# Paged cache of a latent-attention decoder step: cached pages loaded in two layouts instead of transposed on chip

## The chip, the cores and the metric

One core of a Trainium2 chip runs the whole step as one program. The metric is device time of the program in microseconds (us), the median of several executions.

## The reference

One layer of a hybrid decoder, in fp32, for a prompt of 512 tokens and, with the same weights, 8 sample sequences of 8 new tokens each, which have 2048 cached tokens behind them. The layer is: half an FFN, a combined input projection, a convolution branch (A) and a latent attention branch (B), a gated merge, half an FFN. The change touches only the attention of the sample sequences over the cache:

```
ckv = concat(cache_ckv[pages].reshape(2048, 256), ckv_new)   # 16 pages of 128 tokens, by page_table
kpe = concat(cache_kpe[pages].reshape(2048, 32),  kpe_new)
k   = rmsnorm(concat(ckv @ w_uk per head, kpe for all heads))  # per head, 64 + 32 channels
s   = (q . k) * SCALE, causal;  p = softmax(s)
o   = (p @ ckv) @ w_uv per head                                # the latent rows are also the values
```

## The kernel before

**Stages.** FFN 1 (0 to about 400 us), input projections and convolution (to about 640), prompt attention (to about 708), the sample sequences over the cache (708 to 1015), merge, output projection, FFN 2. Matrix products run as three fp32r products of a rounded copy ("hi") and what is left of it ("lo"): hi*hi, hi*lo, lo*hi.

**The cache stage** goes over 8 sequences (`sequences`, L506: sequence 0, a loop for 1 to 4, then 5, 6, 7), each 16 pages in 8 pairs (`pp`). Cached rows `c_nat` come token by channel, one DMA a page, and rope keys `kpe_nat` token by rope channel, another. The pages' numbers are loaded by SyncE from a table (`page_of`, L722). Two halves of `c_nat` (b = 0, 1) alternate between sequences.

For a pair of pages:
- TensorE transposes four 128x128 blocks of `c_nat` into a PSUM bank (`transpose_pair`, L1750), one pair ahead of use;
- ScalarE copies the bank rounded to `cT_hi` (`pages_hi`, L1272), VectorE subtracts, PSUM minus `cT_hi`, to `cT_lo` (`pages_lo`, L2473);
- TensorE multiplies page by page with `kq`, in which the expanded key weights (512 columns) and the absorbed queries (64 columns) stand side by side: 12 matmuls of 288 columns a page (L1868). PSUM banks for pages alternate in two pairs, so page t waits until ScalarE has read page t-2;
- ScalarE copies the scores to `s_buf` (L1327) and squares the keys to `sq` (L1333); VectorE sums the squares per head (L2655).

For a group of four pages the rope keys are transposed by TensorE in one block (`kpe_transpose`, L1815), copied by ScalarE (`kpe_copy`, L1309), and multiplied with the rope queries (`kpe_scores`, L1825); VectorE adds that to the scores (L2663).

**Softmax and values of the sequence before** (r = s - 1) are interleaved as steps of generators (`soft_pe`, `soft_act`, `soft_dve`; each `next(soft)` runs one step at a set page). VectorE: inverse key norms (L2514 to L2519), scaling of the scores (L2524), maxima (L2529, L2532), shift (L2537, L2538). ScalarE: square root (L1286) and exponentials (L1294 to L1299), each with its table load. For sequences 0 to 5 (r) the values are made in hi and lo parts: ScalarE rounds a pair of pages to `c_hi` (`pair_high`, L1303) and GpSimd subtracts, SBUF minus SBUF, to `c_lo` (`split_pair`, L908) in place of `c_nat` (the first four pages go to `c_lo_first`); GpSimd also makes the low parts of the probabilities (L920, L922). The value matmuls (L1778, L1779) stand in two clusters of 16, ahead of pages 12 and 15. The values of the last two sequences are plain fp32 (L1799).

**Other work in the stage**: convolution steps on VectorE (`late_tap`, L2225, both tensors in SBUF) in sequences 1 to 4, layer norm of branch A in 5 to 7.

**Order.** Every engine runs its own instruction list in the order written; waits are on semaphore counts. SyncE alone issues the page DMAs, in order: for sequence 0 eleven pages of `c_nat` early, the rest when `w_uk` is split; for sequence s from 2 on, a group when the splits or the value matmuls of sequence s-2 have used the slot (`load_pages`, L728). Behind them SyncE issues `w_uv` and the merge weights (L758 to L765). `w_uk` and `w_uv` share their place (S3) with `kpe_nat` and `c_lo_first`; `w_uv` is loaded a second time for the end.

Of the kernel before, what the change touches and what calls it, by code (L numbers as in the profile page):

```python
# [22 lines left out]
P = 128  # L23
# [70 lines left out]
def layer(nc, x_t, cols_in, cache_ckv, cache_kpe, state_conv, page_table, w, const, out):  # L94

    ctx = ExitStack()
    with ctx:
# [25 lines left out]
        ones = keep("ones", [P, P], F32)  # L123
        causal = keep("causal", [P, P], F32)
# [110 lines left out]
        c_lo_first = place("c_lo_first", [P, NP // 4, KL], F32R, S3 + 4096)  # L235
        c_lo = place("c_lo", [P, 2, NP, KL], F32R, A0)
# [87 lines left out]
        first_ckv_in, first_kpe_in = [sem(f"first_ckv_in{b}") for b in range(2)], [sem(f"first_kpe_in{b}") for b in range(2)]  # L324
        both_in = [[sem(f"both_in{b}{g}") for g in range(1, NP // 4)] for b in range(2)]
        ckv_in, kpe_in = ([[first[b], *both_in[b]] for b in range(2)] for first in (first_ckv_in, first_kpe_in))

        def landed_pages(g, uses):

            return uses * (128 if g else 64)  # L330

        ct_tr, ct_hi, ct_lo = sem("ct_tr"), sem("ct_hi"), sem("ct_lo")
        page_mm, page_sq, page_red = (sem(n) for n in ("page_mm", "page_sq", "page_red"))

        pe_tr, pe_copied, pe_scored, scores_copied, scores_read = (sem(n) for n in ("pe_tr", "pe_copied", "pe_scored", "scores_copied", "scores_read"))
# [191 lines left out]
        def page_lo(b, t):  # L527

            return c_lo_first[:, t, :] if t < NP // 4 else c_lo[:, b, t, :]
# [63 lines left out]
        def _(sp):  # L593
# [128 lines left out]
            def page_of(s, t):  # L722
                return sp.value_load(pages[0:1, ds(s * NP + t, 1)], min_val=0, max_val=cache_ckv.shape[1] - 1)

            def load_page(src, dst, landed, page, b, t):
                sp.dma_start(dst[:, b, t, :], src[0, ds(page, 1), :, :].rearrange("a p c -> (a p) c")).then_inc(landed[b][t // 4], 16)

            def load_pages(s, b, used=None, split=None):  # L728
                for g in range(NP // 4):
                    if used is not None and g == 0:  # L730
                        sp.wait_ge(split_made, split)
                    elif used is not None:
                        sp.wait_ge(pages_used, used + 2 * (g + 1))
                    for t in range(4 * g, 4 * g + 4):
                        page = page_of(s, t)
                        load_page(cache_ckv, c_nat, ckv_in, page, b, t)
                        load_page(cache_kpe, kpe_nat, kpe_in, page, b, t)

            AHEAD = 11
            sp.wait_ge(prep_q, 1)  # L740
            for t in range(AHEAD):
                load_page(cache_ckv, c_nat, ckv_in, page_of(0, t), 0, t)
            sp.wait_ge(prep_tr, 2)
            sp.wait_ge(uk_split, 1)
            for t in (4, 5, 6, 7, 0, 1, 2, 3):
                load_page(cache_kpe, kpe_nat, kpe_in, page_of(0, t), 0, t)
            for t in range(8, NP):
                page = page_of(0, t)
                if t >= AHEAD:
                    load_page(cache_ckv, c_nat, ckv_in, page, 0, t)  # L750
                load_page(cache_kpe, kpe_nat, kpe_in, page, 0, t)
            sp.wait_ge(prep_mm, 2)
            load_pages(1, 1)
            with sp.Fori(1, NS // 2) as i:
                for b in range(2):
                    load_pages(i * 2 + b, b, i * (2 * PAIRS) + (EARLY_PAIRS + PAIRS * (b - 2)), i * (2 * SPLITS) + (SPLITS * (b - 2) + 2))

            sp.wait_ge(lat_mm, STACKED)  # L758
            sp.dma_start(w_uv[:, :, :], w["w_uv"][0].rearrange("(k p) h d -> p k (h d)", p=P)).then_inc(late_in, 16)
            for t in range(2):  # L760
                load_merge(t)
            sp.wait_ge(page_mm, NS * NP)
# [28 lines left out]
        def _(pool):  # L791
# [116 lines left out]
            def split_pair(r, b, j):  # L908

                two = slice(2 * j, 2 * j + 2)  # L910
                pool.wait_ge(p_done, high_made(r, j))
                pool.tensor_tensor(c_lo_first[:, two, :] if j < 2 else c_lo[:, b, two, :], c_nat[:, b, two, :],
                                   c_hi[j % EARLY_PAIRS][:, :, 0:KL].bitcast(F32), ALU.subtract)\
                    .then_inc(split_made, 1)
# [10 lines left out]
            def squares(s, b, uses, prev, nxt):  # L925
# [10 lines left out]
                for g in range(NP // 4):  # L936
                    pool.wait_ge(kpe_in[b][g], landed_pages(g, uses))
                if prev:
                    pool.wait_ge(kpe_red, s)
                k = kpe_nat[:, b].rearrange("p t d -> p (t d)")  # L940
                pool.tensor_tensor(ta[:, 0:NP * DR], k, k, ALU.mult).then_inc(kpe_sq, 1)
# [13 lines left out]
        def _(act):  # L955
# [347 lines left out]
            def pair_high(r, b, j):  # L1303

                act.wait_ge(ct_tr, r * PAIRS + (j + 1))
                act.wait_ge(pages_used, r * PAIRS + (j + 1))
                act.activation(c_hi[j % EARLY_PAIRS][:, :, 0:KL], c_nat[:, b, 2 * j:2 * j + 2, :], ACT.Copy).then_inc(p_done, 1)

            def kpe_copy(s, g):  # L1309

                act.wait_ge(pe_tr, s * 4 + (g + 1))
                if not (isinstance(s, int) and s == 0 and g < 2):
                    act.wait_ge(pe_scored, s * 4 + (g - 1))
                act.activation(kpeT[:, g % 2, :], ps[:, PEB, 4 * HQ:4 * HQ + P], ACT.Copy).then_inc(pe_copied, 1)

            def act_seq(s, b, uses, prev, nxt):
                soft = soft_act(s - 1, 1 - b) if prev else None
                for pp in range(NP // 2):
                    if pp + 1 < NP // 2 or nxt:
                        pages_hi(s * (NP // 2) + (pp + 1), (pp + 1) % 2)  # L1320
                    if pp == 4 and nxt:
                        queries_hi(s + 1, 1 - b)
                    for u in range(2):
# [10 lines left out]
                        if t == kpe_page(s, t // 4):  # L1334
                            kpe_copy(s, t // 4)
                        if prev and t in (1, 8, 9):
                            next(soft)
                        if prev and stacked(s):
                            if 2 <= t < 2 + EARLY_PAIRS:
                                pair_high(s - 1, 1 - b, t - 2)  # L1340
                            if t - LATE_AT in (0, 1):
                                for j in range(2):
                                    pair_high(s - 1, 1 - b, EARLY_PAIRS + 2 * (t - LATE_AT) + j)
# [72 lines left out]
        def _(pe):  # L1416
# [333 lines left out]
            def transpose_pair(s, b, uses, pp):  # L1750

                n = s * (NP // 2) + pp
                if pp % 2 == 0:
                    pe.wait_ge(ckv_in[b][pp // 2], landed_pages(pp // 2, uses))
                if not (isinstance(s, int) and s == 0 and pp < 2):
# [1027 lines left out]
```

## Time and profile before

| | us |
|---|---|
| median of 3 runs (1528.05 to 1530.12) | 1528.22 |
| the profiled execution | 1529.87 |
| its span, first to last instruction | 1528.0 |
| TensorE busy (99% of the span) | 1513.9 |
| VectorE busy (69%) | 1055.5 |
| ScalarE busy (43%) | 659.7 |
| GpSimd busy (29%) | 448.2 |

How to read it: PE is TensorE's matmuls, PEld its weight loads, DVE VectorE, ACT ScalarE, POOL GpSimd, SP SyncE; an SPq row is an issue by SyncE's queue. A row `out<-in xN` is a group of N instructions; "idle before" is the time the engine waited, with what ended the wait. Matmuls are pipelined and their ends are modelled, so their times overlap and a busy TensorE is not one at its peak. The chain of waits goes back from the last instruction to what released each step. The granted clock is 0.997 over the span, 1.0 being 2.4 GHz.

### The profile page before, as it was taken

The numbers are of one execution on the slowest core, as the hardware profiler recorded it, in microseconds if no ns is written. First come the engines' busy times: TensorE is split into PE (matmuls) and PEld (weight loads), VectorE is DVE, ScalarE is ACT, GpSimd is POOL, SyncE is SP. The second block draws the span as 40 slices with busy tenths as digits, with TensorE's granted clock in tenths as the row PEclk, the third lists the DMA queues.
The fourth block names the chain that finished last, engine by engine and source line by source line (L and its number), as shares of the span: only waits on it lengthen the run. The fifth ranks groups of instructions, "written<-read, shape, count | busy, mean of one in ns | idle before, by whom it ended". The sixth has DMA issues, their size and how long they took to land.

```text
span 1528.0 us, 31401 instructions
## 1 busy us (share of the span) xinstructions
PE 1513.9 (99%) x11059; PEld 1463.9 (96%) x11059; DVE 1055.5 (69%) x1738; ACT 659.7 (43%) x1247; POOL 448.2 (29%) x463
## 2 busy tenths in 40 slices
PE   8999999999999999999999999999999999999999
PEld 8999999999999999588999999988999999999999
DVE  6999898422269975865877787864659998985000
ACT  6444445322221241364666666662434544444111
POOL 4000002454455743320233333223551000005432
PEclk9999999999999999999999999999999999999999
DMA  6233334232323571002322222312222333332322
GB/s 176 70 97 98 94 90 123 66 95 76 82 75 96 94 119 48 1 1 61 76 67 60 66 63 63 89 56 71 83 82 67 99 96 89 103 95 80 90 76 82
DMA packets 239316, 122.82 MB, mean 80 GB/s; under 512 B 37041, under 2 KB 236146, under 8 KB 239218
## 3 DMA queue, kind: packets, MB, share of 16 engines
q1 hardware_dynamic: 238354, 121.09, 29.6%
q8 instruction: 55, 0.90, 0.2%
q10 hardware_dynamic: 864, 0.48, 0.1%
q14 instruction: 43, 0.35, 0.1%
HBM read 117.95 MB, written 3.58 MB: 80 GB/s over the span
## 4 chain that ended last, share of the span: by engine, by line
PE 67%; issue 21%; POOL 7%; DVE 2%; ACT 2%; DMA 1%; SPq 0%; POOLq 0%; ACTq 0%; DVEq 0%
PE ps L490 29%; PE ps L1506 14%; PE ps L1868 11%; POOL w_lobuf L465 7%; PE ps L1760 1%; PE ps L1631 1%; PE ps L1685 1%; PE ps L1660 1%; PE ps L1799 1%; PE ps L1778 1%; PE ps L1828 1%; PE ps L1779 1%; DMA w_rawbuf<-in_ffn_w_gu 1%; PE ps L476 1%; PE ps L1675 1%
## 5 line engine op out<-in xcount | busy, mean ns | idle before, releaser
L465 POOL TENSOR_TENSOR w_lobuf<-w_rawbuf,w_hibuf 128x256 fp32r<-128x256 f32 (+1 forms) x328 | 316.9, 997 | 798.7 <-ACT w_hibuf L458 798.5
L1506 PE MATMUL ps<-xs,w 128*128 128x288 f32 x3192 | 427.4, 296 | 0.8 <-DVE w L1994 0.8
L1506 PEld LDWEIGHTS ps<-xs,w 128*128 128x128 f32 x3192 | 426.8, 188 | 1.3 <-issue 1.3
L458 ACT ACTIVATE w_hibuf<-w_rawbuf 128x1024 fp32r<-128x1024 f32 (+1 forms) x89 | 104.4, 1172 | 348.1 <-PE ps L490 332.9
L2202 DVE SCALAR_TENSOR_TENSOR xT<-ps,xT 128x576 f32<-128x576 f32 x23 | 17.4, 757 | 202.4 <-PE ps L490 202.4
L1994 DVE TENSOR_TENSOR w<-w_raw,w 128x512 fp32r<-128x512 f32 x228 | 153.5, 688 | 1.0 <-ACT w L1006 0.8
L490 PE MATMUL ps<-a_hi,w_lobuf 128*128 128x288 f32 x682 | 147.5, 297 | 0.0
L490 PE MATMUL ps<-x_hi,w_hibuf 128*128 128x288 f32 x656 | 142.6, 299 | 4.6 <-POOL w_lobuf L465 2.7
L490 PE MATMUL ps<-a_hi,w_hibuf 128*128 128x288 f32 x682 | 147.2, 296 | 0.0
L490 PE MATMUL ps<-a_lo,w_hibuf 128*128 128x288 f32 x682 | 145.4, 294 | 0.0
L490 PE MATMUL ps<-x_lo,w_hibuf 128*128 128x288 f32 x656 | 141.3, 297 | 0.0
L490 PE MATMUL ps<-x_hi,w_lobuf 128*128 128x288 f32 x656 | 141.3, 297 | 0.0
L1006 ACT ACTIVATE w<-w_raw 128x512 fp32r<-128x512 f32 x228 | 131.9, 624 | 6.0 <-DVE w_raw L1988 2.4
L1868 PE MATMUL ps<-kq_hi,cT_hi 128*128 128x288 f32 x512 | 117.6, 311 | 1.3 <-ACT sq L1333 0.8
L490 PEld LDWEIGHTS ps<-x_hi,w_hibuf 128*128 128x128 f32 x656 | 105.8, 189 | 6.4 <-POOL w_lobuf L465 4.0
L2225 DVE SCALAR_TENSOR_TENSOR y<-ext,cols,y 128x512 f32<-128x512 f32 x120 | 108.8, 906 | 4.1 <-DVE y L2225 1.4
L490 PEld LDWEIGHTS ps<-a_hi,w_hibuf 128*128 128x128 f32 x682 | 110.2, 189 | 0.0
L1868 PE MATMUL ps<-kq_lo,cT_hi 128*128 128x288 f32 x512 | 109.4, 295 | 0.0
L1868 PE MATMUL ps<-kq_hi,cT_lo 128*128 128x288 f32 x512 | 109.3, 295 | 0.0
L490 PEld LDWEIGHTS ps<-a_lo,w_hibuf 128*128 128x128 f32 x682 | 109.3, 188 | 0.0
L490 PEld LDWEIGHTS ps<-a_hi,w_lobuf 128*128 128x128 f32 x682 | 109.0, 188 | 0.0
L1018 ACT ACTIVATE ta<-ta 128x576 f32<-128x576 f32 x38 | 26.1, 687 | 189.3 <-DVE ta L2093 189.3
(343 smaller groups left out, 2729.6 us busy)
## 6 DMA issues: line engine op xcount, KB each, us to landing
w_raw<-in_ffn_w_gu SPq DMA_DIRECT2D x76, 256.0 KB, 2.9
up_rows<-in_ffn_w_gu SPq DMA_DIRECT2D x72, 256.0 KB, 3.1
c_nat<-in_cache_ckv SPq DMA_DIRECT2D x128, 128.0 KB, 2.0
w_rawbuf<-in_w_in SPq DMA_DIRECT2D x58, 256.0 KB, 3.2
w_rawbuf<-in_ffn_w_down SPq DMA_DIRECT2D x32, 384.0 KB, 4.1
w_rawbuf<-in_ffn_w_down SPq DMA_DIRECT2D x32, 320.0 KB, 3.4
w_rawbuf<-in_ffn_w_gu SPq DMA_DIRECT2D x24, 256.0 KB, 3.4
w_rawbuf<-in_w_out SPq DMA_DIRECT2D x16, 256.0 KB, 3.2
```

Of the source, the lines that this page charges most:

```text
L458: act.activation(w_hibuf[:, r % HIS, 0:size], w_rawbuf[:, r, 0:size], ACT.Copy).then_inc(w_hi_done, 1)
L465: ins = pool.tensor_tensor(w_lobuf[:, r, part], w_rawbuf[:, r, part], w_hibuf[:, r % HIS, part].bitcast(F32), ALU.subtract)
L476: mm = pe.matmul(ps[:, 2 * s + h, 0:HALF], a, b[:, k, h * HALF:(h + 1) * HALF], start=False, stop=i == len(kts) - 1 and j == 2)
L490: mm = pe.matmul(ps[0:width, 2 * s + h, 0:HALF], a, b[:, k, h * HALF:(h + 1) * HALF], start=first and i == 0 and j == 0, stop=last and i = ...
L1006: act.activation(w7[b][:, slot, 0, :], src, ACT.Copy).then_inc(w7_hi, 1)
L1018: act.activation(ta[:, :], ta[:, :], ACT.Silu).then_inc(gate_act, 1)
L1506: mm = pe.matmul(ps[:, seven_bank(f, slot), 0:HALF], m, xs[:, slot, n, k, :], start=k == 0 and j == 0, stop=k == KH - 1 and j == 2)
L1631: mm = pe.matmul(ps[0:n, 2 * s + b, 0:QL], qaT[k][:, i * P:i * P + n], w_uq[:, k, b * QL:(b + 1) * QL], start=k == 0, stop=k == QL // P - 1)
L1868: mm = pe.matmul(ps[:, page_banks(t) + half, 0:KQ], a, m[:, half, cols], start=k == 0 and j == 0, stop=k == 1 and j == 2)
L1994: dve.tensor_tensor(w7[b][:, slot, 1, :], w7_raw[b][:, slot, 1, :], w7[b][:, slot, 0, :].bitcast(F32), ALU.subtract).then_inc(w7_lo, 1)
L2202: dve.scalar_tensor_tensor(x2, unit(s), scale, x2, op0=ALU.mult, op1=ALU.add).then_inc(x_done, 1)
L2225: dve.scalar_tensor_tensor(dst, src, cw, dst, op0=ALU.mult, op1=ALU.add).then_inc(conv_p_step, 1)
```

## The change

The host hands over the cached pages in three arrays: `pages_t` (page, 128 channels, 2 x 128 tokens), `pages_in` (page, token, 256 latent and 32 rope channels) and `pages_k` (page, 32 rope channels, 128 tokens). The kernel no longer gets `cache_ckv` and `cache_kpe`.

- `c_ring`, 8 slots of a page in the place of `w_uk` and `w_uv`, receives `pages_t`. `pages_hi` and `pages_lo` read it instead of PSUM. A group of four pages takes half the ring; it is loaded when `ct_lo` shows the half's pairs split.
- `kpeT` receives `pages_k` directly, four DMAs of 32 partitions a group; `kpe_transpose` and `kpe_copy` go, `kpe_scores` waits for the DMA.
- `c_nat` has rows of 288 and receives `pages_in`, for values and for the squares of the rope keys, which GpSimd now makes in place. `c_lo_first` goes; all of `c_lo` is made in place.
- `transpose_pair` goes with all its calls. ScalarE's `pages_hi` waits for the ring's DMA and for the matmuls of the pair before the last.
- SyncE issues three DMAs a page and loads four page numbers ahead of each group's waits. Its order within a group: ring, rope keys, rows. `w_uv`'s second load moves behind the last `cT_lo`.
- Small tiles are moved to other places (`diag`, `top`, `mx`, `o_lat`, `den_sum`, `o_all[0]`, ...).

```diff
+        c_nat = place("c_nat", [P, 2, NP, KL + DR], F32, A0)
+        RING = 8
+        c_ring = place("c_ring", [P, RING, KL], F32, S3)
+        c_lo = place("c_lo", [P, 2, NP, KL + DR], F32R, A0)
...
+            def load_ring(g, found):
+                for u, page in enumerate(found):
+                    sp.dma_start(c_ring[:, (4 * g + u + RING // 2) % RING, :], pages_t[ds(page, 1), :, :].rearrange("a p c -> (a p) c"))\
+                        .then_inc(ring_in[g % 2], 16)
+            def load_rows(b, g, found):
+                for u, page in enumerate(found):
+                    sp.dma_start(c_nat[:, b, 4 * g + u, :], pages_in[ds(page, 1), :, :].rearrange("a p c -> (a p) c")).then_inc(nat_in[b][g], 16)
+            def load_kpe(g, found):
+                for u, page in enumerate(found):
+                    sp.dma_start(kpeT[u * DR:(u + 1) * DR, g % 2, :], pages_k[ds(page, 1), :, :].rearrange("a d t -> (a d) t")).then_inc(kpe_in[g % 2], 16)
+            def load_pages(s, b, used=None):
                 for g in range(NP // 4):
+                    found = [page_of(s, 4 * g + u) for u in range(4)]
+                    sp.wait_ge(ct_lo, s * PAIRS + (2 * g - 2))
+                    load_ring(g, found)
+                    sp.wait_ge(pe_scored, s * (NP // 4) + (g - 1))
+                    load_kpe(g, found)
+                    if used is not None:
                         sp.wait_ge(pages_used, used + 2 * (g + 1))
+                    load_rows(b, g, found)
...
+            sp.wait_ge(rows_done, 2 * NT + PT_TILES)
+            found = [page_of(0, u) for u in range(4)]
+            load_ring(0, found)
+            load_kpe(0, found)
             sp.wait_ge(prep_q, 1)
+            load_rows(0, 0, found)
+            for g in (1, 2):
+                load_rows(0, g, [page_of(0, 4 * g + u) for u in range(4)])
             sp.wait_ge(prep_tr, 2)
             sp.wait_ge(uk_split, 1)
+            found = [page_of(0, 4 + u) for u in range(4)]
+            load_ring(1, found)
+            load_kpe(1, found)
+            load_rows(0, 3, [page_of(0, 12 + u) for u in range(4)])
...
             sp.wait_ge(lat_mm, STACKED)
-            sp.dma_start(w_uv[:, :, :], ...).then_inc(late_in, 16)
             for t in range(2):
                 load_merge(t)
+            sp.wait_ge(ct_lo, NS * PAIRS)
+            sp.dma_start(w_uv[:, :, :], ...).then_inc(late_in, 16)
...
-                pool.tensor_tensor(ta[:, 0:NP * DR], k, k, ALU.mult).then_inc(kpe_sq, 1)
+                k = c_nat[:, b, :, KL:KL + DR]
+                pool.tensor_tensor(k, k, k, ALU.mult).then_inc(kpe_sq, 1)
...
-            def pages_hi(n, b):
-                act.wait_ge(ct_tr, n + 1)
-                act.activation(cT_hi[:, b, :], ps[:, b, :], ACT.Copy).then_inc(ct_hi, 1)
+            def pages_hi(s, pp):
+                act.wait_ge(ring_in[pp // 2 % 2], (s * 2 + (pp // 4 + 1)) * 64)
+                if not (isinstance(s, int) and s == 0 and pp < 2):
+                    act.wait_ge(page_mm, s * NP + (2 * pp - 2))
+                act.activation(cT_hi[:, pp % 2, :], ring_pair(pp), ACT.Copy).then_inc(ct_hi, 1)
...
-                tr.then_inc(ct_tr, 1)          # transpose_pair, all of it
-                    .then_inc(pe_tr, 1)        # kpe_transpose, all of it
+                pe.wait_ge(kpe_in[g % 2], (s * 2 + (g // 2 + 1)) * 64)     # kpe_scores
...
-                dve.tensor_tensor(cT_lo[:, b, :], ps[:, b, :], cT_hi[:, b, :].bitcast(F32), ALU.subtract).then_inc(ct_lo, 1)
+                dve.tensor_tensor(cT_lo[:, pp % 2, :], ring_pair(pp), cT_hi[:, pp % 2, :].bitcast(F32), ALU.subtract).then_inc(ct_lo, 1)
```

## Rows read from the trace of the kernel before

**Rows 1.** Busy times by stretch: sequence 1, 5, 6.
```profile
core 0: us, PE busy (x) PEld busy (x) DVE busy (x) ACT busy (x) POOL busy (x), PEclk, DMA share, GB/s
745.40:782.70 37.30, 37.03 (x281) 35.90 (x279) 29.08 (x50) 25.43 (x63) 14.36 (x12) 1.00 0.22 57
...
894.70:935.40 40.70, 38.94 (x287) 37.19 (x286) 31.25 (x54) 27.12 (x68) 14.81 (x12) 1.00 0.23 59
935.40:972.80 37.40, 36.60 (x279) 35.60 (x277) 29.99 (x50) 26.23 (x66) 14.32 (x12) 1.00 0.25 64
```

**Rows 2.** Chain of waits in sequence 0: start, us, engine, line.
```profile
725.34 0.11 PE ps L1822
725.45 0.44 PE ps L1760 x4
725.88 3.17 PE ps L1868 x24
```

**Rows 3.** Chain of waits in sequence 2, pages 8 and 11.
```profile
801.43 0.34 ACT L1294
...
804.53 1.59 PE ps L1868 x10
```

**Rows 4.** Chain of waits in sequences 5 and 7.
```profile
906.77 2.08 DVE mx L2529
...
999.11 7.05 PE ps L1799 x32
```

**Rows 5.** Chain of waits at the start of sequence 0.
```profile
708.35 1.04 PE ps L1760 x4
```

**Rows 6.** Busy times by stretch: just before sequence 0.
```profile
704.40:707.80 3.40, 3.40 (x19) 3.40 (x17) 2.45 (x5) 0.00 (x0) 0.00 (x0) 0.50 0.08 12
```

**Rows 7.** Timeline of VectorE, sequence 2: start, us, instruction, idle before.
```profile
789.28 0.69 DVE L2475 TENSOR_TENSOR cT_lo<-ps,cT_hi 128x512 fp32r<-128x512 f32 x1 [1.61 <-ACT cT_hi L1275]
...
792.54 0.68 DVE L2475 TENSOR_TENSOR cT_lo<-ps,cT_hi 128x512 fp32r<-128x512 f32 x1
...
801.49 0.20 DVE L2538 TENSOR_TENSOR s_buf<-s_buf,ps 64x64 f32<-64x64 f32 x1
...
806.47 0.69 DVE L2475 TENSOR_TENSOR cT_lo<-ps,cT_hi 128x512 fp32r<-128x512 f32 x1 [1.28 <-ACT cT_hi L1275]
807.08 0.78 DVE L2225 SCALAR_TENSOR_TENSOR y<-ext,cols,y 128x512 f32<-128x512 f32 x1
...
810.83 1.28 DVE L2225 SCALAR_TENSOR_TENSOR y<-ext,cols,y 128x512 f32<-128x512 f32 x1
```

**Rows 8.** Timeline of ScalarE, sequence 2, after page 8.
```profile
801.43 1.28 ACT L1294 ACT_TABLE_LOAD   x1
```

**Rows 9.** Timeline of GpSimd, sequence 2.
```profile
790.44 2.87 POOL L912 TENSOR_TENSOR c_lo_first<-c_nat,c_hi 128x512 fp32r<-128x512 f32 x2 [11.78 <-ACT c_hi L1307]
...
806.03 1.27 POOL L920 TENSOR_TENSOR p_two<-s_buf,p_two 128x512 fp32r<-128x512 f32 x1 [0.79 <-ACT s_buf L1299]
...
809.21 2.34 POOL L912 TENSOR_TENSOR c_lo<-c_nat,c_hi 128x512 fp32r<-128x512 f32 x2 [1.18 <-ACT c_hi L1307]
```

**Rows 10.** Timeline of SyncE's queue: issues in sequence 2, and behind the pages.
```profile
812.07 0.34 SPq L726 DMA_DIRECT2D c_nat<-in_cache_ckv  x1
812.59 0.33 SPq L726 DMA_DIRECT2D kpe_nat<-in_cache_kpe  x1
813.75 0.34 SPq L726 DMA_DIRECT2D c_nat<-in_cache_ckv  x1
...
985.61 0.47 SPq L615 DMA_DIRECT2D w_rawbuf<-in_w_conv_out  x1
```

**Rows 11.** Line 726, all issues: ns min/median/max, first and last start.
```profile
L726 SPq DMA_DIRECT2D kpe_nat<-in_cache_kpe x128: 332/333/1604, 705.5 to 984.6; - x128
```

**Rows 12.** Waits of SyncE's queue: waited for, us, times, longest.
```profile
SPq L723 <- PE ps L1779: 51.3, 6, 10.1
```

**Rows 13.** DMA issues: KB each, median us to landing.
```profile
c_nat<-in_cache_ckv SPq DMA_DIRECT2D x128, 128.0 KB, 2.0
```

More of the change, by code:

```diff
@@ L91, in constants, with layer @@
     return {"ident": ident, "causal": causal, "rope": rope, "new_mask": new}
-def layer(nc, x_t, cols_in, cache_ckv, cache_kpe, state_conv, page_table, w, const, out):
+def layer(nc, x_t, cols_in, pages_t, pages_in, pages_k, state_conv, page_table, w, const, out):
     ctx = ExitStack()
@@ L323, in layer, with ring_pair @@
         ukT_done = sem("ukT_done")
[L324 to L332, printed above, removed]
+        nat_in = [[sem(f"nat_in{b}{g}") for g in range(NP // 4)] for b in range(2)]
+        ring_in = [sem(f"ring_in{g}") for g in range(2)]
+        kpe_in = [sem(f"kpe_in{g}") for g in range(2)]
+        def ring_pair(pp):
+            at = (2 * pp + RING // 2) % RING
+            return c_ring[:, at:at + 2, :].rearrange("p t c -> p (t c)")
+        ct_hi, ct_lo = sem("ct_hi"), sem("ct_lo")
         page_mm, page_sq, page_red = (sem(n) for n in ("page_mm", "page_sq", "page_red"))
-        pe_tr, pe_copied, pe_scored, scores_copied, scores_read = (sem(n) for n in ("pe_tr", "pe_copied", "pe_scored", "scores_copied", "scores_read"))
+        pe_scored, scores_copied, scores_read = (sem(n) for n in ("pe_scored", "scores_copied", "scores_read"))
         q_hi_done, q_split = sem("q_hi_done"), sem("q_split")
@@ L527, in page_lo @@
         def page_lo(b, t):
-            return c_lo_first[:, t, :] if t < NP // 4 else c_lo[:, b, t, :]
+            return c_lo[:, b, t, 0:KL]
         def pair_made(r, j):
@@ L722, in page_of @@
             def page_of(s, t):
[L723 to L728, printed above, removed]
-                for g in range(NP // 4):
-                    if used is not None and g == 0:
-                        sp.wait_ge(split_made, split)
-                    elif used is not None:
-                        sp.wait_ge(pages_used, used + 2 * (g + 1))
[L734 to L737, printed above, removed]
@@ L747, in _ @@
[L747 to L751, printed above, removed]
+            found = [page_of(0, 4 + u) for u in range(4)]
+            load_ring(1, found)
+            load_kpe(1, found)
+            load_rows(0, 3, [page_of(0, 12 + u) for u in range(4)])
+            for g in (2, 3):
+                found = [page_of(0, 4 * g + u) for u in range(4)]
+                sp.wait_ge(ct_lo, 2 * g - 2)
+                load_ring(g, found)
+                sp.wait_ge(pe_scored, g - 1)
+                load_kpe(g, found)
@@ L911, in split_pair @@
                 pool.wait_ge(p_done, high_made(r, j))
-                pool.tensor_tensor(c_lo_first[:, two, :] if j < 2 else c_lo[:, b, two, :], c_nat[:, b, two, :],
+                pool.tensor_tensor(c_lo[:, b, two, 0:KL], c_nat[:, b, two, 0:KL],
                                    c_hi[j % EARLY_PAIRS][:, :, 0:KL].bitcast(F32), ALU.subtract)\
@@ L1747, in new_scores @@
                     .then_inc(prep_mm, 1)
[L1750 to L1755, printed above, removed]
-                    pe.wait_ge(ct_lo, n - 1)
-                for u in range(2):
-                    for k in range(2):
-                        c = (2 * u + k) * P
-                        tr = pe.transpose(ps[:, pp % 2, c:c + P], c_nat[:, b, 2 * pp + u, k * P:(k + 1) * P], ident[:, :])
-                tr.then_inc(ct_tr, 1)
             def soft_pe(r, b):
@@ L2756, in laid_out @@
     taps = np.asarray(inputs["conv_w"])[0].T.reshape(CT, P, W).transpose(1, 0, 2).reshape(P, CT * W)
-    return {"x_t": rows.T, "cols_in": np.concatenate([*gains, taps], axis=1)}
+    ckv, kpe = np.asarray(inputs["cache_ckv"])[0], np.asarray(inputs["cache_kpe"])[0]
+    pages_t = ckv.transpose(0, 2, 1).reshape(-1, KL // P, P, PAGE).transpose(0, 2, 1, 3).reshape(-1, P, KL)
+    return {"x_t": rows.T, "cols_in": np.concatenate([*gains, taps], axis=1), "pages_t": pages_t,
+            "pages_in": np.concatenate([ckv, kpe], axis=2), "pages_k": kpe.transpose(0, 2, 1)}
 def state_first(state):
```

85 lines of the change are left out of this document (29 added, 56 removed).

## The prediction, made before the result was known

> **What bounds the kernel now.** I read the page first: TensorE is busy nearly the whole span, so a transpose that goes can be worth time only where the chain of waits runs over TensorE. Next the busy times by sequence of cached pages, then the chain inside them. The work on the cache is eight sequences of 16 pages (8 pairs each); sequences 1 to 4 take 37.3 us each, VectorE is busy 29.1 of that and ScalarE 25.4 [rows 1]. The reader is to see three kinds of sequence. In sequence 0 the chain is TensorE and nothing else: four transposes of a pair take 0.44 us of it, one rope transpose 0.11 [rows 2]. In sequences 1 to 4 the chain leaves TensorE once, for ScalarE's Exp table and the exponentials, and returns at page 11 [rows 3]. In sequences 5 and 6 the first half of the chain is VectorE, which also does the layer norm there [rows 4]. The trace's mean times of matmuls overlap, so I take transposes by their stretch in the chain.
>
> **The transposes.** Removed are 64 pairs x 0.44 and 32 rope transposes x 0.11: 28.2 + 3.5 = 31.7 us of TensorE, 8 x 0.44 + 4 x 0.11 = 4.0 in each sequence. That is the ceiling; the rest is what each sequence gives back.
>
> **Sequence 0** has a bare TensorE chain, few jobs on VectorE and no splits on GpSimd: all 4.0 stay. At its start the first pair's transposes (1.04) stood ahead of ScalarE's first copy [rows 5]; that copy can now start as soon as the projection before it ends. But TensorE ran at the 1.2 GHz level there [rows 6], and with eight transposes less it does less until page 0. Bounds: 1.0 gained, or 3.2 lost if pair 0's 24 matmuls (3.17 at 2.4 GHz [rows 2]) all run at the lower level. I take 0.5 gained: page 0 follows within 2 us.
>
> **Sequences 1 to 4.** Take pages 0 to 10. From the low part of pair 2 (789.28) to the end of the softmax shift (801.49 + 0.20 = 801.69) VectorE has no idle time left: 12.4 us of its own work [rows 7]. TensorE, relieved of five pairs' and three rope transposes (2.5), runs into it. What VectorE waits for at its head, 1.61 us for the rounded copy of pair 2 [rows 7], shrinks by about 0.64, an estimate: 0.44 for the transposes ahead of page 1 and 0.2 for ScalarE's rope copy that no longer stands ahead of the Sqrt table load. So the shift ends at about 801.05. Before, it was not last: ScalarE's table load ended at 801.43 + 1.28 = 802.71 [rows 8], 1.02 after the shift. Now that load comes earlier with page 8 and the exponentials start at the shift. Page 11, which waits for them, starts 1.02 + 0.64 = 1.66 earlier where TensorE alone would give 2.5.
>
> **The new source of VectorE's low parts.** cT_lo was PSUM minus SBUF and becomes SBUF minus SBUF. Rows first: the low part at 806.47 ran beside a GpSimd subtraction (806.03 to 807.30) and took its usual 0.69; the convolution step at 810.83, both of whose tensors lie in SBUF, took 1.28 where the one at 807.08 took 0.78, and ended about 0.55 after GpSimd's two subtractions (809.21 + 2.34 = 811.55) [rows 7, 9]. So an operation with both tensors in SBUF waits until shortly (0.2) before GpSimd's running one ends. In the old positions pair 3's low part (792.54) would stand beside the first two splits (until 793.31): 0.57; pair 6's (806.47) beside the probabilities' low parts (until 807.30): 0.63. Pairs 4, 5 meet nothing; pairs 7 and 0 would wait too, but behind the 16 value matmuls of page 12 and page 15, which cover them; without that cover some 0.9 more. Bounds 0 and 1.2 a meeting (a whole GpSimd operation of 2.34 / 2); I take 0.6 at each of the two. The first delays the shift: page 11 is 1.66 - 0.6 = 1.06 early. The second falls on pair 6. Its low part ended at 806.47 + 0.69 = 807.16, just as the transposes ahead of the pair did, so taking these away uncovers it: the pair starts when the low part is done, 1.06 - 0.63 = 0.4 earlier. Pairs 6 and 7 give their own 0.44 + 0.44 + 0.11 = 1.0. Sum 1.4 of 4.0 a sequence, 1.66 + 1.0 = 2.7 if nothing meets. The Trainium skill says in "SBUF — State Buffer", section "SBUF: two separate sides", that VectorE and GpSimd share one pair of ports under an exclusive lock, and that a VectorE operation with two SBUF inputs contends for it where one with a PSUM input would not. The 1.28 beside the 0.69 agrees; by that rule 1.4 stands, without it 2.7.
>
> ScalarE reads SBUF instead of PSUM for the rounded copies: I take no difference (its 25.4 of 37.3 leaves room; if it were 0.05 dearer, a sequence loses at most that twice). The added waits of ScalarE for pair pp-2's matmuls are already met by the score copy before them. TensorE's rope scores now wait for a DMA, with the next pair's matmuls queued behind them; it is issued a group (13 us) ahead and lands like the pages, so I take nothing; unhidden it is 2.0 a group. In-place squares and the strided sum keep their counts.
>
> **SyncE's queue.** Before, a page costs one load of its number and two DMAs: DMA to DMA 0.52, and 1.16 across a number, so a number costs 0.64 [rows 10]. Now it is three DMAs: 16 x 0.64 + 48 x 0.52 = 10.2 + 25.0 = 35.2 us a sequence, against 26.9. One issue in a while is slow, up to 1.60 instead of 0.33 [rows 11]; with one such (1.2) it is 36.4. SyncE had 51.3 us of waits for used pages in six sequences [rows 12], so it had room; now 36.4 stands against 37.3 - 1.4 = 35.9. A ring half is free once its pairs are split and wanted three pairs later, with 2.0 us to land [rows 13], so a late queue shows as late pages. Bounds of a sequence's gain: 2.7 (no meeting, free queue) and, for issues of 0.60, -2.9. I take 0.9: 4 x 0.9 = 3.6. In sequence 1 the queue starts from the moment w_uk is free and has sequence 0's remaining DMAs ahead: 0.5 lost there, once. Volume: 288 KB a page against 144, so 57 GB/s at a share of 0.22 [rows 1] becomes some 117 at 0.45; no wait by itself.
>
> **Sequences 5 to 7.** In 5 the chain holds three pairs' transposes, two behind VectorE's part and one ahead (1.3), and rope work of 0.4: 1.7, less one meeting of 0.6 and half of another: 0.7. In 6 TensorE holds more of the second half, four pairs and three rope transposes: 1.8 + 0.3 = 2.1, less 0.6: 1.5. In 7 no splits run, the chain is TensorE from pair 2 on: five pairs, 2.2. Moved on SyncE: the first merge weights, issued at 985.61 [rows 10], now stand behind the last ring's rope and row loads, which wait for page 7 of sequence 7; I put them at 994, landing near 998, four late for ScalarE's split after pair 4. The 32 value matmuls of 7.05 us at 999.11 [rows 4] cover that; without them 4 would be lost. w_uv follows the last low part and is used only after the merge's first products: nothing.
>
> **Sum.** 4.0 + 0.5 - 0.5 + 3.6 + 0.7 + 1.5 + 2.2 = 12.0. The profiled execution took 1529.87 (span 1528.0 and 1.9 around it): 1517.9. It lies 1.65 above the median of 1528.22, so I forecast 1516.2.
>
> **Rivals.** First, neither port nor queue binds: GpSimd's work falls elsewhere once the pace changes, and the queue's slow issues go. 4.0 + 1.0 + 4 x 2.7 + 1.7 + 2.1 + 2.2 = 21.8: 1506.4. For it: only two of the meetings are on the path, and SyncE's nominal 35.2 almost fits 37.3 - 2.7 = 34.6. Against: the 1.28. Second, TensorE alone counts: 31.7 + 1.0: 1495.5. Against it the 12.4 us without a gap on VectorE. Third, slower: SyncE's queue sets the pace. At 0.54 a DMA (10.2 + 1.2 + 48 x 0.54 = 37.3) sequences 1 to 4 gain nothing; the whole turns slower from about 0.57. At 0.60 a sequence is 40.2: 4 x 2.9 + 2.8 for sequence 6, less 4.0, 0.5 and 2.2: 7.7 lost, 1535.9. For it: half as many issues again on a queue that has had no such run; against: 0.52 is steady over both kinds of page DMA. Fourth, no change, issues of 0.55 to 0.57: near 1527.
>
> **How the numbers follow.** Forecast 0.53, its own range 1511 to 1521; first rival 0.25; second 0.05; third 0.11; fourth 0.06. A change under 0.2% (3 us) can't be told from none. Faster 0.83, same 0.06, slower 0.11. The range 1505 to 1528 leaves out the second and third and a little of the first.
>
> **What would show it.** Right: no transposes of pages in the trace; sequence 0 near 33.4; sequences 1 to 4 near 36.4; low parts of 1.1 to 1.3 us beside GpSimd's subtractions, at pairs 3 and 6; SyncE with no long wait from sequence 1 to 4; page 11 released by the shift. Wrong: low parts always near 0.69 (no meeting), sequences of 35 or less (queue free), ScalarE's rounded copy waiting for a DMA in every sequence (queue binds, third rival), or the first pages of sequence 0 at 1.2 GHz for long.

## The result and the profile after

The changed kernel takes 1535.24 us against 1529.67 us, both medians of 20 runs: a ratio of 1.0037, 95% interval 1.0028 to 1.0046. It is slower by some 5.6 us where 12.0 less were forecast. The profiled execution has a span of 1531.5 us, 3.5 more than before.

The page of the changed kernel, shares of the chain that ended last by engine: SyncE's queue, which had none before, now holds 11%.

```profile
PE 52%; issue 24%; SPq 11%; POOL 7%; DVE 3%; ACT 1%; DMA 1%; POOLq 0%; DVEq 0%; ACTq 0%
```

The stage is cut from one start of the softmax's maximum on VectorE (`mx`) to the next, so that a stretch is a sequence's length; the last one ends with the loop. Busy times by stretch, changed kernel (columns as in [rows 1]):

```profile
750.59:788.19 37.60, 34.18 (x243) 32.00 (x243) 31.63 (x52) 24.85 (x61) 15.18 (x13) 1.00 0.45 128
788.19:825.47 37.28, 34.09 (x243) 31.93 (x243) 31.35 (x52) 24.82 (x61) 15.13 (x13) 1.00 0.43 128
825.47:866.05 40.58, 35.76 (x243) 33.45 (x243) 31.89 (x52) 24.73 (x61) 15.12 (x13) 0.96 0.43 126
866.05:904.23 38.18, 33.98 (x243) 31.90 (x243) 33.99 (x54) 25.25 (x60) 15.32 (x13) 1.00 0.44 129
904.23:945.47 41.24, 35.18 (x249) 32.98 (x249) 32.10 (x53) 27.06 (x66) 14.88 (x13) 1.00 0.40 116
945.47:984.16 38.69, 35.40 (x249) 32.97 (x249) 33.09 (x53) 25.03 (x62) 11.73 (x10) 1.00 0.43 125
984.16:1017.90 33.74, 29.87 (x170) 24.99 (x171) 20.54 (x33) 19.43 (x39) 7.55 (x9) 0.90 0.35 100
```

The same cut of the kernel before:

```profile
755.69:793.14 37.45, 37.18 (x281) 36.06 (x281) 29.11 (x52) 25.49 (x64) 14.35 (x13) 1.00 0.24 61
793.14:830.38 37.24, 36.95 (x281) 35.83 (x280) 29.34 (x53) 25.37 (x64) 14.66 (x13) 1.00 0.26 65
830.38:867.79 37.41, 37.16 (x281) 36.04 (x280) 29.08 (x53) 25.48 (x64) 14.34 (x13) 1.00 0.25 64
867.79:906.70 38.91, 38.09 (x288) 36.77 (x287) 31.49 (x55) 26.21 (x66) 15.38 (x14) 1.00 0.26 66
906.70:947.33 40.63, 38.78 (x288) 37.05 (x287) 30.56 (x54) 27.57 (x70) 14.80 (x13) 1.00 0.23 60
947.33:985.85 38.52, 38.22 (x287) 36.91 (x286) 31.59 (x53) 25.49 (x66) 10.72 (x10) 1.00 0.25 63
985.85:1014.77 28.92, 28.88 (x188) 24.37 (x187) 20.19 (x33) 19.79 (x42) 7.08 (x9) 1.00 0.19 56
```

The projection of the queries ahead of the first page, before and changed:

```profile
702.79 5.55 PE L1737 MATMUL ps<-qT_new,w_ukT 64*128 64x64 f32 x32
701.41 3.73 PE L1753 MATMUL ps<-qT_new,w_ukT 64*128 64x64 f32 x32
```

The reader is to see four things. The first maximum comes 5.10 earlier (750.59 for 755.69), but 1.38 of that lies ahead of anything that changed, since the projection starts that much earlier; sequence 0 and its start gave 3.7. TensorE is then 3 us less busy in a sequence, and the sequence is no shorter for it: TensorE filled 37 of 37.3 us before and fills 34 now, while VectorE rose from 29.2 to 31.6. One sequence is 3.17 longer, and the last stretch 4.82. Sum: -5.10 + 0.15 + 0.04 + 3.17 - 0.73 + 0.61 + 0.17 + 4.82 = +3.13 at the loop's end, and +0.4 after it. Without the 1.38 that is 4.9, nearer to the 5.6 of the medians.

The long sequence, in the chain of waits (start, us, engine and line; SPq is SyncE's queue):

```profile
830.23 0.33 SPq L737
...
833.41 0.34 SPq L731
...
839.23 0.33 SPq L737
839.74 2.65 issue
...
845.27 0.35 SPq L731
```

Between two groups stand the four page numbers: 3.18 from the last row load (830.23) to the next ring load (833.41), 2.66 of it for the numbers. At 839.74 SyncE does nothing for 2.65: that is the jump back of its loop (line 778), and the next ring load comes 6.04 after the last row load. The second jump, at 917.24, takes 3.06. The kernel before has such a jump too, and SyncE stands there for 2.48 the first time, between these two issues, and for 2.64 the second:

```profile
830.26 0.33 SPq L726 DMA_DIRECT2D kpe_nat<-in_cache_kpe  x1
834.24 0.35 SPq L726 DMA_DIRECT2D c_nat<-in_cache_ckv  x1
```

There it cost nothing that shows: the stretch from 830.38 takes 37.41, like those ahead of it. In the changed kernel TensorE runs dry behind the first jump, and its granted clock falls from 2.4 to 1.2 GHz (busy times by stretch, changed kernel):

```profile
849.00:851.00 2.00, 0.44 (x4) 0.21 (x2) 1.16 (x2) 1.23 (x3) 0.00 (x0) 1.00 0.30 66
...
853.00:855.00 2.00, 2.00 (x8) 1.82 (x8) 1.13 (x3) 1.07 (x3) 0.00 (x0) 0.50 0.00 1
```

SyncE has nearly no wait left from 700 to 1010 us, against 51.3 us for used pages [rows 12]:

```profile
SPq L765 <- DVE kq_lo L2460: 3.3, 1, 3.3
SPq L742 <- PE ps L1825: 3.0, 2, 2.5
```

The last stretch, chain of waits of the changed kernel, and TensorE's clock there by stretch:

```profile
995.91 0.40 SPq L618
996.36 4.82 DMA w_rawbuf<-in_w_conv_out
...
1002.28 1.28 ACT L1387
...
1004.35 0.62 ACT cT_hi L1300
...
1008.23 5.59 PE ps L1861 x24
...
1014.09 3.38 PE ps L1861 x24
```

```profile
1005.00:1008.00 3.00, 0.44 (x4) 0.42 (x4) 3.00 (x3) 3.00 (x7) 2.40 (x4) 0.71 0.00 0
1008.00:1010.00 2.00, 2.00 (x9) 1.99 (x10) 2.00 (x5) 1.13 (x2) 2.00 (x3) 0.50 0.01 4
```

The merge weights are issued 10.3 later than before [rows 10] and land at 1001.18. ScalarE waits 6.1 us for them with pair 6's rounded copy behind; TensorE works off its value matmuls, runs dry, and then makes 24 products in 5.59 at 1.2 GHz that take 3.38 at 2.4.

### The profile page after: what moved, and what is told of

It reads as the page before. It is cut to its first block, busy times and chain, and to the rows that moved or that the text cites. A ratio compares the mean times of both kernels' runs of the same rounds, so it can differ in the third digit from the quotient of the medians.

```text
span 1531.5 us, 31143 instructions
## 1 busy us (share of the span) xinstructions
PE 1491.3 (97%) x10771; PEld 1434.9 (94%) x10771; DVE 1067.9 (70%) x1738; ACT 655.5 (43%) x1215; POOL 454.3 (30%) x463
## 4 chain that ended last, share of the span: by engine, by line
PE 52%; issue 24%; SPq 11%; POOL 7%; DVE 3%; ACT 1%; DMA 1%; POOLq 0%; DVEq 0%; ACTq 0%
PE ps L493 28%; PE ps L1522 14%; POOL w_lobuf L468 7%; SPq L726 3%; SPq L731 3%; SPq L742 3%; SPq L737 2%; PE ps L1861 2%; PE ps L1647 1%; PE ps L1701 1%; PE ps L1676 1%; PE ps L479 1%; PE ps L1691 1%; DMA w_rawbuf<-in_ffn_w_gu 1%; DVE cT_lo L2466 1%
## 5 line engine op out<-in xcount | busy, mean ns | idle before, releaser
L1861 PEld LDWEIGHTS ps<-kq_hi,cT_hi 128*128 128x128 f32 x512 | 84.1, 194 | 25.3 <-DVE cT_lo L2466 10.4
```

The source lines that it names most:

```text
L1861: mm = pe.matmul(ps[:, page_banks(t) + half, 0:KQ], a, m[:, half, cols], start=k == 0 and j == 0, stop=k == 1 and j == 2)
```

## The experiments

Theory A: SyncE's queue sets the pace. Theory B: the compute engines do, with VectorE's low parts stretched beside GpSimd, and the queue only runs level with them. Ratios are to the kernel before, with 95% intervals; the changed kernel stands at 1.0037. Differences between two kernels are those of their ratios, times 1529.6 us.

**e1, a longer queue.**

```diff
-found = [page_of(s, 4 * g + u) for u in range(4)]
+found = [page_of(s, 4 * g + u) for u in (0, 0, 1, 2, 3)][1:]
```

> The changed kernel with one more load of a page number in each group of four pages (five for four; the fifth number is not used). In the trace of the changed kernel a group of the loop (four numbers, twelve transfers) takes SyncE 9.0 to 9.7 us without a wait, and one number about 0.65 us. Theory A, SyncE's issue sets the pace of sequences 1 to 7: 28 groups x 0.65 = 18.2 us more, less some 3 us of waits of SyncE that are left in the stage, so 15 to 18 us above the changed kernel, 1550 to 1553 us. Theory B, the compute engines set the pace (VectorE with low parts stretched beside GpSimd) and SyncE only runs level with them: 0 to 3 us, 1535 to 1538 us.

1551.87 us, 1.0144 (1.0128 to 1.0160): 16.4 more, as A said. There is no room in the queue. A sequence without a jump takes 39.14 (793.49 to 832.63), one with a jump 44.79 at a mean clock of 0.92:

```profile
832.63:877.42 44.79, 37.05 (x243) 34.74 (x243) 31.48 (x52) 24.85 (x61) 15.12 (x13) 0.92 0.40 113
```

**e2, a shorter queue.**

```diff
-found = [page_of(s, 4 * g + u) for u in range(4)]
+found = nc.values_load_multi_w_load_instructions(
+    pages[0:1, ds(s * NP + 4 * g, 4)], engines=[mybir.EngineType.SP],
+    ..., skip_runtime_bounds_check_because=...)[1]
```

> The changed kernel with the four page numbers of a group fetched by one load instruction without range checks, in place of four loads with two register instructions each; every transfer is the same. The four took 2.6 us in a group of 9.0. Theory A: a group falls to 6.9 to 8.3 us, SyncE's 28 to 33 us a sequence come under what TensorE and VectorE need (34.5 to 36 us by low parts and chain), and the loop's two jumps are covered too: 1510 to 1520 us, and SyncE waits again in most groups. Theory B: 1533 to 1536 us.

1526.11 us, 0.9979 (0.9970 to 0.9987): 8.9 less than the changed kernel and faster than the kernel before, but 6 above what A gave. SyncE waits again, 60 us for rope scores:

```profile
SPq L747 <- PE ps L1830: 60.0, 21, 7.2
```

The edit took away more than the numbers' time. The loop's jump back, 2.65 and 3.06 in the changed kernel, takes 0.24 and 0.23 here. Around the first of them 1.41 pass from the last row load (833.96) to the next ring load, where it was 6.04:

```profile
832.37 1.92 SPq L742 DMA_DIRECT2D c_nat<-in_pages_in  x4
835.37 1.89 SPq L736 DMA_DIRECT2D c_ring<-in_pages_t  x4
```

So the 8.9 are the price of numbers and jumps together, with what hangs on them in the tail. And yet a sequence takes what it took before:

```profile
788.74:825.91 37.17, 34.02 (x243) 31.94 (x243) 32.41 (x52) 25.00 (x61) 15.08 (x13) 1.00 0.46 131
```

So B holds for the plain sequences. With the queue out of the way the engines need 37.15 us; the changed kernel's queue lay level with that and cost time only where it fell behind and could not catch up.

**e3, the jumps.**

```diff
-with sp.Fori(1, NS // 2) as i:
-    for b in range(2):
-        load_pages(i * 2 + b, b, i * (2 * PAIRS) + (EARLY_PAIRS + PAIRS * (b - 2)))
+for s in range(2, NS):
+    load_pages(s, s % 2, EARLY_PAIRS + PAIRS * (s - 2))
```

> The changed kernel with SyncE's loop over sequences 2 to 7 written out; the same transfers and numbers in the same order. In the trace of the changed kernel SyncE stands for 2.7 us after each of the loop's two jumps back (839.7 and near 917 us). Theory A: two jumps x 2.8 = 5.6 us less, 1529 to 1530 us. Theory B: no change, 1535 us.

1528.82 us, 0.9998 (0.9988 to 1.0008): 6.0 less, about what A said. The sequence of the jump takes 37.14 like its neighbours, TensorE's clock stays at 2.4 GHz from sequence 1 on, and ScalarE's wait for the merge weights falls from 6.1 to 3.9, since all later issues come earlier.

```profile
827.22:864.36 37.14, 34.01 (x243) 31.95 (x243) 32.32 (x53) 25.09 (x61) 15.11 (x13) 1.00 0.44 127
```

The jumps are not all that went. Written out, a group without a slow issue takes SyncE 8.4, as in sequence 1, which stands outside the loop in both kernels; in the loop it takes 9.0 (ring loads from 824.41 to 833.41). From the last row load to the next ring load it is 2.7 where the loop takes 3.2. The ring loads of two groups of e3:

```profile
831.69 1.89 SPq L731 DMA_DIRECT2D c_ring<-in_pages_t  x4
840.09 1.88 SPq L731 DMA_DIRECT2D c_ring<-in_pages_t  x4
```

No run parts the jumps from this. What the first jump alone cost is read from its stretch in the changed kernel, 40.58 for 37.41 before and 37.14 in e3: 3.2 to 3.4.

**e4, the merge weights ahead of the last group**, on top of e3.

```diff
+if (s, g) == (NS - 1, 2):
+    sp.wait_ge(lat_mm, STACKED)
+    for t in range(2):
+        load_merge(t)
```

> As e3_unrolled_queue, and the first two loads of merge weights issued inside sequence 7, ahead of the pages of its last group, instead of behind all of its pages; in the changed kernel ScalarE waited 6.1 us for them there. If the late weights cost time of their own: 3 to 5 us less than e3_unrolled_queue, 1525 to 1527 us. If that wait lay beside the queue's own delay: the same as e3, or up to 2 us more, since four more transfers stand ahead of the last group of the ring.

1527.74 us, 0.9989 (0.9979 to 0.9999): the intervals of e3 and e4 overlap, so this run settles nothing by its time: 1.4 less by the ratios, where 3 to 5 or none was expected.

**e7, the merge weights alone**: loop and numbers as in the changed kernel, the four transfers moved to another queue.

```diff
-for t in range(2):
-    load_merge(t)          # SyncE, behind all pages
+if at(s, pp) == (NS - 1, 1):   # ScalarE, sequence 7
+    act.wait_ge(lat_mm, STACKED)
+    ...
+    act.dma_start(dst[...], wc[...]).then_inc(w_in_sem[...], 16)
```

> The changed kernel, SyncE's loop and its numbers as they were, with the first two loads of merge weights issued by ScalarE in sequence 7 ahead of its pair 1's squares instead of by SyncE behind all pages. From the last maximum of the loop's sequences to the end of the sequences the changed kernel takes 4.8 us more than the kernel before, 5.5 more than e2, and ScalarE waits 6.1 us for these weights there. If the late weights are the cause: 4 to 5 us less than the changed kernel, 1530 to 1531 us. If the tail is late for another reason (the queue behind the second jump, the lower clock by itself): 1534 to 1536 us.

1532.32 us, 1.0015 (1.0004 to 1.0025): 3.4 less than the changed kernel, somewhat under the 4 to 5 expected. This overlaps with e3's 6.0, in which the weights come earlier too; the two are not to be added. In its tail TensorE stays busy at 2.4 GHz:

```profile
1006.00:1010.00 4.00, 4.00 (x20) 2.55 (x19) 4.00 (x5) 3.93 (x7) 3.41 (x4) 1.00 0.01 2
```

**e5, the meetings on the ports.** In e2 of the low parts seen from 745 to 985 us, 20 of 51 take 1.41 in the mean and the others 0.68; in the kernel before, all 50 took 0.68 (as at 806.47 in [rows 7], beside GpSimd's 806.03 in [rows 9]). Timeline of VectorE and of GpSimd in e2, sequence 2 to 3:

```profile
800.96 1.35 DVE L2471 TENSOR_TENSOR cT_lo<-c_ring,cT_hi 128x512 fp32r<-128x512 f32 x1 [1.16 <-ACT cT_hi L1305]
...
805.41 1.52 DVE L2471 TENSOR_TENSOR cT_lo<-c_ring,cT_hi 128x512 fp32r<-128x512 f32 x1
...
807.77 1.60 DVE L2220 SCALAR_TENSOR_TENSOR y<-ext,cols,y 128x512 f32<-128x512 f32 x1 [0.18 <-DVE y L2220]
...
810.49 1.49 DVE L2471 TENSOR_TENSOR cT_lo<-c_ring,cT_hi 128x512 fp32r<-128x512 f32 x1
```

```profile
800.49 1.28 POOL L950 TENSOR_TENSOR p_two<-s_buf,p_two 128x512 fp32r<-128x512 f32 x1 [0.64 <-ACT s_buf L1329]
...
804.03 2.35 POOL L942 TENSOR_TENSOR c_lo<-c_nat,c_hi 128x512 fp32r<-128x512 f32 x2 [1.54 <-ACT c_hi L1337]
807.63 2.79 POOL L942 TENSOR_TENSOR c_lo<-c_nat,c_hi 128x512 fp32r<-128x512 f32 x2 [1.25 <-ACT c_hi L1337]
810.39 1.03 POOL L969 TENSOR_TENSOR c_nat<-c_nat 128x512 f32<-128x512 f32 x1
```

These are pairs 6 and 7 and, at 810.49, pair 0 of the next sequence; pair 3 is the fourth long one. Pair 6 stands beside the probabilities, pairs 3 and 7 beside splits, and pair 0 beside the squares of the rope keys (810.39), which come right behind the splits. Each ends 0.55 after the GpSimd operation beside which it started (pair 0: 811.98 behind 811.43). The convolution step at 807.77 waits too; it did so in the kernel before, where it took 1.28 ([rows 7], 810.83).

```diff
-pool.tensor_tensor(c_lo[:, b, two, 0:KL], c_nat[:, b, two, 0:KL], c_hi[...][:, :, 0:KL]...)
+pool.tensor_tensor(c_lo[:, b, two, 0:8], c_nat[:, b, two, 0:8], c_hi[...][:, :, 0:8]...)
-mm = pe.matmul(ps[:, 7, 0:KL], two, page_lo(b, t), ...)
+mm = pe.matmul(ps[:, 7, 0:KL], two, c_hi[j % EARLY_PAIRS][:, u, 0:KL], ...)
```

> e2_numbers_at_once with GpSimd's low parts of the value pages cut to 8 of 256 channels; TensorE multiplies by the rounded pages a second time in their place, so the matmuls are as many and as long (what is left out: the low parts of the values of sequences 0 to 5). In e2 a sequence takes 37.15 us without any wait of SyncE's, and four of its eight low parts of pages on VectorE take 1.32 to 1.52 us beside a running GpSimd operation instead of 0.68; three of the four stand beside these splits. Theory P, the meetings of VectorE and GpSimd set that pace: 1.5 to 2.9 us less in each of six sequences, 9 to 17 us under e2, 1509 to 1517 us. Theory C, the pace is the chain from rounded copy over low part, products and squares by itself and the meetings lie in its gaps: at most 3 us under e2, 1523 to 1526 us.

1518.04 us, 0.9928 (0.9914 to 0.9942): 7.8 less than e2, between the two theories. Six long low parts are left, all beside the probabilities; pair 0's is short again, since the squares come earlier, and the convolution step takes 0.75. A sequence takes 35.63:

```profile
789.70:825.33 35.63, 33.49 (x246) 31.88 (x244) 29.51 (x53) 24.84 (x60) 6.62 (x12) 1.00 0.46 134
```

The three low parts and the convolution step cost 1.5 us a sequence together, about half of what VectorE is busier with them (32.4 for 29.5). How the 1.5 divide among the four isn't shown.

**e9 and e10, the transposes put back** on e2 and on e5, results unused.

```diff
+pe.wait_ge(nat_in[b][pp // 2], uses * 64)
+for u in range(2):
+    for k in range(2):
+        c = (2 * u + k) * P
+        pe.transpose(ps[:, pp % 2, c:c + P], c_nat[:, b, 2 * pp + u, k * P:(k + 1) * P], ident[:, :])
```

> e2_numbers_at_once with the 32 page transposes of a sequence put back on TensorE (sequences 1 to 7, ahead of each pair's products, from the pages loaded token by channel into the two PSUM banks that the change left free); nothing reads them. With e2 and the next two it makes a square: transposes or none, GpSimd's splits or none. In e2 TensorE is busy 34.0 of 37.15 us of a sequence, and 32 transposes were priced at 4.0 us. If the transposes' removal was worth something in spite of the meetings: 38 to 38.6 us a sequence, 6 to 10 us above e2, 1532 to 1536 us. If all of it went into TensorE's idle time behind VectorE: 0 to 3 us above e2, 1526 to 1529 us.

> e5_small_splits with the same transposes put back; left out as there: the low parts of the values of sequences 0 to 5. e5 takes 35.65 us a sequence with TensorE busy 33.5. If TensorE then sets the pace as in the kernel before (37.24 us, 99% busy): 37.2 to 37.6 us a sequence, 11 to 13 us above e5, 1529 to 1531 us. That would put the worth of the transposes at 11 to 13 us without the meetings, and at the difference of e9 and e2 with them. If a chain through VectorE sets it: 0 to 4 us above e5.

e9: 1530.31 us, 1.0004 (0.9995 to 1.0014), 3.8 above e2. e10: 1526.77 us, 0.9984 (0.9975 to 0.9993), 8.6 above e5. A sequence of e9 and one of e10:

```profile
791.11:828.96 37.85, 36.76 (x277) 35.40 (x276) 32.38 (x52) 24.93 (x59) 14.77 (x13) 1.00 0.45 126
```

```profile
789.25:827.07 37.82, 36.73 (x277) 35.30 (x276) 29.52 (x53) 24.76 (x60) 6.61 (x12) 1.00 0.43 127
```

With the transposes TensorE is busy 36.7 and a sequence takes 37.9 with the splits and 37.7 without, in the mean of the first three stretches. Without the transposes it is 37.15 with the splits and 35.65 without. Both fall between my cases: the page transposes of sequences 1 to 7 are worth 8.6 us where GpSimd's splits are cut and 3.8 where VectorE meets them.

**e6, e8 and e11, a version with both costs lowered.** e6 makes GpSimd's splits and squares wait for VectorE's low parts, on e2; e8 adds e3 and e4; e11 is e8 with these waits in sequences 1 to 4 only.

```diff
 pool.wait_ge(p_done, high_made(r, j))
+if not isinstance(r, int):        # e11 only
+    pool.wait_ge(ct_lo, (r + 1) * PAIRS + (3, 4, 4, 5, 7, 8, 8, 8)[j])
...
+if nxt:                           # e11: if not isinstance(s, int)
+    pool.wait_ge(ct_lo, (s + 1) * PAIRS + 1)
 k = c_nat[:, b, :, KL:KL + DR]
```

> e2_numbers_at_once with GpSimd's splits and its squares of the rope keys made to wait for the low part of the next pair on VectorE, so that they run between two low parts; nothing is left out. Theory P: three of four meetings gone, 1.0 to 2.1 us less in a sequence, 6 to 12 us under e2, 1514 to 1520 us; less if the values of page 15 then wait for the last split. Theory C: 1524 to 1528 us.

> The changes of e2, e4 and e6 together: four numbers by one load, SyncE's loop written out, the merge weights ahead of the last group, GpSimd's splits between the low parts. Theory P: 6 to 13 us under e2, 1513 to 1520 us. Theory C: 1523 to 1527 us. Since e2 has the queue out of the way already, loop and merge weights give 0 to 2 us here beyond e6.

> e8_all_and_splits_wait with GpSimd's waits for VectorE's low parts kept in sequences 1 to 4 only. In e6 the sequences 1 to 4 came down from 37.15 to 36.4 us, but the two after them, where VectorE has the layer norm as well, went up by 2.2 and 0.8 us. Expected by that: 3 to 4 times 0.75 us below e2, with 0 to 1 us for the merge weights: 1522 to 1524 us. If the splits' shift only moves the wait to the values: 1525 to 1527 us.

e6: 1526.04 us, 0.9976 (0.9965 to 0.9988), no gain on e2 where 6 to 12 were expected. Of 50 low parts 12 stay long, at pairs 6 and 0. Sequences 1 to 4 fall to 36.4, and one later on takes 43.31 for e2's 41.08. e8: 1525.78 us, 0.9981 (0.9967 to 0.9995), the same. e11: 1523.48 us, 0.9963 (0.9949 to 0.9976), as expected and the fastest that computes everything, some 6 us under the kernel before and 11 under the changed one. In the loop a sequence takes 36.41 (787.05 to 823.46); one behind it:

```profile
898.06:940.76 42.70, 36.76 (x249) 34.43 (x249) 32.56 (x53) 26.95 (x66) 15.36 (x13) 0.96 0.41 116
```

That is 1.6 above e2's 41.08, though it has no such waits: TensorE stood idle for most of the time from 923 to 925 and was granted 1.2 GHz from 927 to 929; e2, idle in the like place too, kept 2.4 GHz. What made the difference was not tried.

## Why the prediction was wrong, point by point

Two steps carry the miss. The queue was taken to lie level with the engines and its loop's jump was put at nothing: 8.9 us with what goes with it. And the gains were put at 12.0 where, with the queue's cost out of the way in e2, 3.2 came: VectorE, with its low parts waiting beside GpSimd, took TensorE's place, and the first pages ran at 1.2 GHz.

- **Sequence 0 and its start**: near in sum, wrong in its parts. 4.5 were forecast, 0.5 of them given back at the start of sequence 1; from the start of the projection to the first maximum 3.72 came, and 2.47 in e2. The term that failed is the clock, where 0.5 gained was taken out of 1.0 gained to 3.2 lost. Page 0 did follow 1.6 after the projection, 1.1 sooner than before, but the first two pairs' products took 9.28 in the changed kernel and 8.49 in e2, where 24 of them take 3.17 at 2.4 GHz [rows 2]. The granted clock stood at 1.2 GHz, the sign that the prediction itself gave for being wrong:

```profile
706.78 9.28 PE ps L1861 x48
708.53 8.49 PE ps L1866 x48
707.00:709.00 2.00, 2.00 (x9) 2.00 (x10) 1.94 (x4) 0.16 (x1) 0.00 (x0) 0.50 0.71 194
```

  (Chain of waits of the changed kernel and of e2; busy times by stretch of the changed kernel.) Half of the changed kernel's 3.72 is luck of the execution: its projection kept 2.4 GHz and took 3.73, where the same projection took 5.76 in e2 and 5.56 in e7, and 5.55 in the kernel before.
- **Sequences 1 to 4**: wrong, and this holds apart from the queue. The step took 1.4 a sequence by VectorE's chain (35.9 us) and 0.9 with the queue. With waits left in the queue, e2's four stretches are 37.18, 37.17, 37.15 and 38.19: gains of 0.27, 0.07, 0.26 and 0.72, the last of which reaches into sequence 5. The mis-sized term is the meetings. Two of 0.6 were put on the path, and "pairs 7 and 0 would wait too, but behind the 16 value matmuls of page 12 and page 15, which cover them; without that cover some 0.9 more". Four a sequence take 0.73 more each. e5 shows that those that go with the splits, pairs 3, 7 and 0 and the convolution step, cost 1.5 where 0.6 was put, so the cover was not there; that is 0.9 of the 1.25 by which 35.9 was short. The other 0.35 is open; the convolution step, which waits 0.32 longer in e2 than in the kernel before and was put at nothing, may be part of it. The mechanism was right: a low part that starts beside GpSimd takes 1.41, one alone 0.68. The Trainium skill's "SBUF — State Buffer", section "SBUF: two separate sides", agrees with that.
- **Sequences 5 to 7**: wrong; 0.7, 1.5 and 2.2 were put (the first is 0.8 by its own terms, 1.7 - 0.6 - 0.3), and e2 gives -0.45, -0.15 and 0.72 (41.08, 38.67 and 28.20). The step took four to five pairs' transposes off the chain. In e5 and e10, without the splits, the fifth and sixth stretch differ by 0.43 and 0.45 only (39.09 for 39.52, 38.17 for 38.62): e5's chain runs over ScalarE and VectorE with its layer norm up to 901.9, e10's over TensorE, and the two come out nearly alike, so the transposes had little to give. The splits cost these two stretches 2.0 and 0.5 (e2 against e5). How this divides between meetings and layer norm wasn't tried.
- **SyncE's queue**: the step compared 36.4 with 35.9 and let the larger set the pace. Its parts were sized well: 0.52 a DMA, 2.66 for four numbers where 0.64 each were put, and 9.0 a group in the loop, 36.0 a sequence where 35.2 was put ahead of slow issues. What failed is that the loop's jump was put at nothing. It costs nothing while SyncE has waits to give up, as in the kernel before; in the changed kernel the first jump's 2.65 made its sequence 3.2 longer. The second, 3.06, hardly lengthens its own stretch (41.24, e2 41.08) and is found again in the late weights of the tail. e3 takes both away, with the loop's register instructions: 6.0 us.
- **The clock after a stall**: not in the sum. Behind the late ring load at 845.27 and the late weights TensorE ran dry and its granted clock fell to 1.2 GHz, so that more was paid than the stall, 2.2 us in the tail (5.59 - 3.38).
- **Merge weights**: "The 32 value matmuls of 7.05 us at 999.11 [rows 4] cover that; without them 4 would be lost." Issue and landing were put at 994 and 998 and came at 995.91 and 1001.18. The matmuls covered TensorE, not ScalarE, whose Silu and rounded copy of pair 6 stood behind the waiting split. e7 prices it at 3.4.
- **The third rival** gave 1535.9, and 1535.24 was measured, but not by its price: it wanted 0.60 a DMA in every sequence, and the DMAs kept 0.52. Direction and engine were its own; the place was the jumps and the tail.

Of the 17.6 us between forecast and result, e2 against the changed kernel puts 8.9 on the queue (jumps and merge weights in it). The other 8.8, from the 12.0 forecast to e2's 3.2, are by the stretches above 1.5 in sequence 0 and the starts (4.0 forecast, 2.47 come), 2.3 in sequences 1 to 4 and 4.3 in 5 to 7; the 0.7 left is the difference between one profiled execution and the medians. What makes 35.65 of e5's sequence where TensorE is busy 33.5 was not tried.

## What to carry to other kernels

An engine that has been waiting hides its own overheads. Before a change uses up its waits, add up every instruction it runs, loop jumps and register loads too, and not just its DMAs. A relief of the bound engine is worth what the next one leaves: ask which operand moves between memories with the change, and whom the new one meets. A stall ahead of TensorE costs more than its own length when the granted clock falls behind it. Two profiled executions can differ ahead of all that changed, so measure a stage from a start that both kernels share.

## What the runs showed of the hardware

SyncE stood for 2.65 and 3.06 us at its loop's jumps back, for 2.48 and 2.64 in the kernel before and for 0.24 and 0.23 in e2; written out the stream has no such gap. The loop's body is 437 recorded instructions long in the changed kernel, 329 before and 325 in e2, so the length alone does not tell which jump stalls. The Trainium skill's "Runtime: NRT & Kernel Launch", section "Instruction fetch mechanics", has a taken branch wait for its target to be fetched if that lies outside the window held; the rows agree with a stall at the jump, and no run here shows that it is the fetch. With one load instruction for four page numbers in place of four loads and their range checks, and the shorter jumps that came with it, SyncE had 60 us of waits again over seven sequences. A VectorE operation with both tensors in SBUF that started beside a GpSimd operation ended 0.55 us after it, 1.41 us long in the mean for 0.68.
